# FFN up tiles: high and low parts of the input side by side in one matmul of 512 columns

## What is computed

```python
def conv_ffn(h, w_up, conv_w, conv_b, w_down):      # w_up 1024 x 5632, w_down 2816 x 1024
    u = dwconv(h @ w_up, conv_w, conv_b)            # depthwise over tokens, 3 taps, zero padded
    gate, val = jnp.split(u, 2, axis=-1)
    return (jax.nn.silu(gate) * val) @ w_down

lat = lat + g2 * conv_ffn(hl, ffn_w_up, ffn_conv_w, ffn_conv_b, ffn_w_down)
```

## Time and profile before

| | |
|---|---|
| median of 3 runs | 872.07 us |
| the profiled execution | 871.97 us, of it the span from first to last instruction 870.2 us |
| FFN stage: first up matmul to the start of the last down tile | 276.9 to 465.0 us of the span |
| TensorE busy | 859.8 us, 99% of the span |
| VectorE busy | 657.1 us, 76% |
| ScalarE busy | 488.6 us, 56% |
| DMA | 160.9 MB, 185 GB/s on average |

### The profile page before, as it was taken

How to read it: one execution, slowest core, us unless ns; L and a number is a source line. 1 busy time by engine, 2 the same in 40 slices (tenths; PEclk the granted TensorE clock), 3 DMA queues, 4 the chain that set the end, 5 groups by cost and what they waited for, 6 DMA issues and landing times.

```text
span 870.2 us, 16530 instructions
## 1 busy us (share of the span) xinstructions
PE 859.8 (99%) x6054; PEld 768.5 (88%) x6054; DVE 657.1 (76%) x1118; ACT 488.6 (56%) x774; POOL 0.2 (0%) x4
## 2 busy tenths in 40 slices
PE   8999999999999999999999999999999999999997
PEld 3688888888899999999998899999998888888886
DVE  4793899999997788877668797766577767666665
ACT  5433677777765654555557545555545555444444
POOL 0000000000000000000000000000000000000000
PEclk9999999999999999999999999999999999999999
DMA  9974444444446657556564554444465456555551
GB/s 346 408 290 154 148 144 147 145 145 145 165 153 237 193 201 249 177 199 192 170 196 142 199 189 147 152 164 147 145 218 168 128 192 214 193 193 183 181 191 49
DMA packets 45441, 160.90 MB, mean 185 GB/s; under 512 B 5200, under 2 KB 6608, under 8 KB 45264
## 3 DMA queue, kind: packets, MB, share of 16 engines
q1 hardware_dynamic: 43488, 156.43, 52.7%
q10 hardware_dynamic: 1904, 3.81, 1.2%
HBM read 159.16 MB, written 1.05 MB: 184 GB/s over the span
## 4 chain that ended last, share of the span: by engine, by line
PE 93%; DVE 3%; ACT 2%; DMA 1%; issue 1%; SPq 1%; DVEq 0%; ACTq 0%
PE bank L418 19%; PE bank L420 18%; PE bank L419 18%; PE bank L439 6%; PE bank L483 5%; PE bank L485 5%; PE bank L484 5%; PE bank L440 3%; PE bank L1232 2%; PE bank L1236 2%; PE bank L1240 2%; DMA arena<-in_ada 1%; PE bank L451 1%; PE bank L1358 1%; PE bank L1201 1%
## 5 line engine op out<-in xcount | busy, mean ns | idle before, releaser
L412 DVE TENSOR_TENSOR w_lo<-raw,w_hi 128x1024 fp32r<-128x1024 f32 x244 | 295.1, 1223 | 100.9 <-ACT w_hi L405 100.7
L405 ACT ACTIVATE w_hi<-raw 128x1024 fp32r<-128x1024 f32 x244 | 252.7, 1051 | 92.2 <-PE bank L420 45.1
L418 PE MATMUL bank<-h_both,w_hi 128*128 128x256 f32 (+1 forms) x928 | 281.2, 303 | 0.0
L419 PE MATMUL bank<-h_both,w_hi 128*128 128x256 f32 (+1 forms) x928 | 276.2, 298 | 0.0
L420 PE MATMUL bank<-h_both,w_lo 128*128 128x256 f32 (+1 forms) x928 | 275.9, 297 | 0.0
L418 PEld LDWEIGHTS bank<-h_both,w_hi 128*128 128x128 f32 x928 | 174.4, 188 | 8.2 <-issue 1.3
L420 PEld LDWEIGHTS bank<-h_both,w_lo 128*128 128x128 f32 x928 | 175.0, 189 | 5.7
L419 PEld LDWEIGHTS bank<-h_both,w_hi 128*128 128x128 f32 x928 | 174.8, 188 | 5.2
L418 PE MATMUL bank<-y_hi,w_hi 128*128 128x256 f32 x304 | 87.0, 286 | 0.1
L419 PE MATMUL bank<-y_lo,w_hi 128*128 128x256 f32 x304 | 85.6, 281 | 0.0
L420 PE MATMUL bank<-y_hi,w_lo 128*128 128x256 f32 x304 | 85.5, 281 | 0.0
(11 more groups left out here) (283 smaller groups left out, 1194.9 us busy)
## 6 DMA issues: line engine op xcount, KB each, us to landing
raw<-in_stream SPq DMA_DIRECT2D x244, 512.0 KB, 3.4
arena<-in_ada SPq DMA_DIRECT2D x40, 512.0 KB, 7.2
xres<-in_ada SPq DMA_DIRECT2D x8, 512.0 KB, 3.3
tok<-in_tok SPq DMA_DIRECT2D x4, 512.0 KB, 5.4
con<-in_con ACTq DMA_DIRECT2D x1, 1472.0 KB, 6.2
xres<-in_tok ACTq DMA_DIRECT2D x1, 1024.0 KB, 8.4
out<-arena SPq DMA_DIRECT2D x4, 256.0 KB, 2.0
arena<-in_post_mix ACTq DMA_DIRECT2D x1, 512.0 KB, 4.1
```

The lines of the kernel that those rows point to most:

```text
L405: act.activation(w_hi[c.slot][:, :], raw[c.slot][:, :], ACT.Copy).then_inc(S("split_hi"), 1)
L412: dve.tensor_tensor(w_lo[c.slot][:, :], raw[c.slot][:, :], w_hi[c.slot][:, :].bitcast(F32), ALU.subtract).then_inc(S("split_lo"), 1)
L418: pe.matmul(dst, hi_w, a_hi, start=start, stop=False, skip_group_check=True)
L419: pe.matmul(dst, hi_w, a_lo, start=False, stop=False, skip_group_check=True)
```

## The change

The up tiles of steps 1 to 21 use `apart_tile`; those of step 0 put their low products into the right half of the bank. ScalarE copies the right half to SBUF (`z_low`), VectorE adds the left half from PSUM to it (`z_f`), and both the convolution's starter on ScalarE and VectorE's taps read `z_f` from SBUF. TensorE's wait before up(j) is for the adds of tile j - 2, one for each half. The gate sums follow the steps 2, 4, ..., 16, and 18 steps are written out. SP issues the fifth to the eighth gate load behind the stream groups 3, 5, 7 and 8.

```diff
-GATE_ROWS = (0, 0, 1, 1, 1, 1, 1, 1, 1, 1)
+GATE_ROWS = (0, 0) + (1, 0) * 8
-FFN_PEEL = 10
+FFN_PEEL = 18
+GATE_GROUPS = (3, 5, 7, 8)
@@ arena
+        z_low = [part(T) for _ in range(2)]
+        z_f = [part(T) for _ in range(2)]
+        used[0] = TC + 8 * T
@@ SP
-            for u in range(1, 5):
+            for u in range(1, 9):
                 load_stream(i_ffn + u)
-                for k in (2 * u - 2, 2 * u - 1) if u >= 3 else ():
-                    load_gate(k)
-            with sp.Fori(i_ffn + 5, N_ALL // RING) as i:
+                if u in GATE_GROUPS:
+                    load_gate(4 + GATE_GROUPS.index(u))
+            with sp.Fori(i_ffn + 9, N_ALL // RING) as i:
                 load_stream(i)
@@ ScalarE, ffn_tile
-                act.wait_ge(S("multiplied"), n_done)
+                for half in range(2):
+                    act.wait_ge(S("multiplied"), n_done + half - 1)
+                    if has_old:
+                        act.wait_ge(S("z_full"), t * 2 + half - 1)
+                    act.activation(z_low[half], psum[4 + 2 * half + p][:, T:2 * T], ACT.Copy).then_inc(S("z_low"), 1)
                 if has_old:
                     act.wait_ge(S("u_full"), t - 1)
                 for half in range(2):
-                    act.activation(conv[p][half], psum[4 + 2 * half + p][:, 0:T], ACT.Identity,
+                    act.wait_ge(S("z_full"), t * 2 + (1 + half))
+                    act.activation(conv[p][half], z_f[half], ACT.Identity,
                                    scale=p1("conv_w", t + (2 * JF + half * JF)),
                                    bias=p1("conv_b", t + half * JF)).then_inc(S("conv_mid"), 1)
@@ TensorE, ffn_up
                 if has_old:
-                    pe.wait_ge(S("conv"), j * 2 - 2)
-                column_tile(pe, c[0], psum[4 + p][:, 0:T], T, T)
-                column_tile(pe, c[1], psum[6 + p][:, 0:T], T, T)
+                    pe.wait_ge(S("z_full"), j * 2 - 3)
+                apart_tile(pe, c[0], psum[4 + p])
+                if has_old:
+                    pe.wait_ge(S("z_full"), j * 2 - 2)
+                apart_tile(pe, c[1], psum[6 + p])
@@ VectorE, ffn_tile
                 for half in range(2):
-                    z = psum[4 + 2 * half + p]
+                    dve.wait_ge(S("z_low"), t * 2 + (1 + half))
+                    dve.tensor_tensor(z_f[half], psum[4 + 2 * half + p][:, 0:T], z_low[half], ALU.add).then_inc(S("z_full"), 1)
+                for half in range(2):
                     x = conv[p][half]
                     dve.wait_ge(S("conv_mid"), t * 2 + (1 + half))
-                    dve.scalar_tensor_tensor(x[:, 1:T], z[:, 0:T - 1], p1("conv_w", t + half * JF), x[:, 1:T],
-                                             ALU.mult, ALU.add).then_inc(S("conv_left"), 1)
+                    dve.scalar_tensor_tensor(x[:, 1:T], z_f[half][:, 0:T - 1], p1("conv_w", t + half * JF), x[:, 1:T],
+                                             ALU.mult, ALU.add).then_inc(S("conv"), 1)
```

More of the change, by code:

```diff
@@ L993, in ffn_tile @@
                     between()
-                act.wait_ge(S("conv"), t * 2 + 2)
+                act.wait_ge(S("conv"), t * 4 + 4)
                 act.activation(f_silu[p], conv[p][0], ACT.Silu).then_inc(S("f_silu"), 1)
@@ L1450, in ffn_up @@
                 if first:
-                    first_columns_late(pe, c, [psum[4][:, 0:T], psum[6][:, 0:T]], 2 * KT)
+                    first_columns_late(pe, c, [psum[4][:, 0:T], psum[6][:, 0:T]], 2 * KT, [psum[4][:, T:2 * T], psum[6][:, T:2 * T]])
                     return
                 if has_old:
-                    pe.wait_ge(S("conv"), j * 2 - 2)
-                column_tile(pe, c[0], psum[4 + p][:, 0:T], T, T)
-                column_tile(pe, c[1], psum[6 + p][:, 0:T], T, T)
+                    pe.wait_ge(S("z_full"), j * 2 - 3)
[3 more added lines that the diff above has]
+                apart_tile(pe, c[1], psum[6 + p])
             def ffn_down(t, s, c, first, last):
@@ L2037, in ffn_tile @@
                 for half in range(2):
-                    z = psum[4 + 2 * half + p]
+                    dve.wait_ge(S("z_low"), t * 2 + (1 + half))
+                    dve.tensor_tensor(z_f[half], psum[4 + 2 * half + p][:, 0:T], z_low[half], ALU.add).then_inc(S("z_full"), 1)
+                for half in range(2):
                     x = conv[p][half]
                     dve.wait_ge(S("conv_mid"), t * 2 + (1 + half))
-                    dve.scalar_tensor_tensor(x[:, 1:T], z[:, 0:T - 1], p1("conv_w", t + half * JF), x[:, 1:T],
-                                             ALU.mult, ALU.add).then_inc(S("conv_left"), 1)
+                    dve.scalar_tensor_tensor(x[:, 1:T], z_f[half][:, 0:T - 1], p1("conv_w", t + half * JF), x[:, 1:T],
+                                             ALU.mult, ALU.add).then_inc(S("conv"), 1)
                 for half in range(2):
-                    z = psum[4 + 2 * half + p]
                     x = conv[p][half]
-                    dve.wait_ge(S("conv_left"), t * 2 + (1 + half))
-                    dve.scalar_tensor_tensor(x[:, 0:T - 1], z[:, 1:T], p1("conv_w", t + (4 * JF + half * JF)), x[:, 0:T - 1],
+                    dve.wait_ge(S("conv"), t * 4 + (1 + half))
+                    dve.scalar_tensor_tensor(x[:, 0:T - 1], z_f[half][:, 1:T], p1("conv_w", t + (4 * JF + half * JF)), x[:, 0:T - 1],
                                              ALU.mult, ALU.add).then_inc(S("conv"), 1)
-                dve.wait_ge(S("conv"), t * 2 + 2)
+                dve.wait_ge(S("conv"), t * 4 + 4)
                 dve.wait_ge(S("f_silu"), t + 1)
```

## The result

| | before | after |
|---|---|---|
| median | 872.07 us (871.95 to 872.6, 4 runs) | 888.52 us (888.21 to 890.79, 4 runs) |
| ratio after / before | | 1.0194, 95% interval 1.018 to 1.0207 |
| the profiled execution | 871.97, span 870.2 | 890.79, span 889.0 |
| start of down(21) in it | 465.04 | 481.30 |

The change costs 16.4 us, 1.9%. The forecast was 884.8 with a range of 879 to 890: the direction and the mechanism were right, the size 3.7 us short.

The account below looks back on a forecast made before the run. TensorE's matmuls bound the kernel, but VectorE with ScalarE would become slower: 22 tiles at 1.14 us hide TensorE's 3.4 us gain and start the last down tile 12.8 us later. 871.97 + 12.8 = 884.8 us, range 879 to 890.

Parts of the forecast that it names:

- up(j): The two up tiles of FFN step j on TensorE; expected to wait on VectorE's low parts from about step 3 on.
- down(21): The last FFN down tile on TensorE; forecast to start at 477.8 instead of 465.04, 12.8 us later.
- the ring: VectorE and ScalarE's ordered chain between closing subtractions; forecast 8.6 us a plain step, 9.8 with gate sum, over TensorE's 8.48.
- close(j-2) - 0.6: Earliest stall-free start of step j's up tiles: 0.6 us before VectorE's closing subtraction of tile j-2.
- d: Time added per FFN tile by VectorE's adds and the starters now waiting for them: 1.14 us, over 22 tiles.
- close(21): VectorE's closing subtraction of the last FFN tile; forecast at 477.3, against 463.87 before the change.
- upper bound of 1.25: Highest d considered, in us a tile: a starter of 0.65 and hand-overs twice as long.
- lower bound 0.79: Lowest d considered, in us a tile: only the two adds' issue on VectorE, starters hidden.
- rival C: ScalarE's convolution starters stay hidden, d is 0.79, 7.7 us less: 877.1 us; chance 5%.
- rival B: VectorE's taps get shorter reading SBUF, 0.425 each, 4.4 us less: 880.4 us; chance 6%.
- rival A: TensorE stays the bound in the FFN, adds and starters fall into waits, only -3.4 us remains: 868.6 us; chance 8%.
- rival D: TensorE's clock falls in the wait before the last down tile, up to 2.9 us more there: about 888; chance 12%.

Follow-up runs that it names:

- three_matmuls: The changed kernel with three matmuls of 256 columns in place of one of 512 and one of 256: 889.59 us.
- wait_moved: The changed kernel with ScalarE's wait for u_full moved from between the low-half copies and the starters to ahead of the copies: 887.96 us.
- adds_ahead: The changed kernel with ScalarE's low-half copies and VectorE's two adds moved ahead of the step's second weight chunk: 876.29 us.
- spread_only: The kernel before with only the gate sums spread to steps 2 to 16, their loads moved and 18 steps written out: 872.19 us.
- short_sums: The changed kernel with each gate sum on 8 of its 1024 columns, waits and loads kept: 881.70 us.
- pieces: The changed kernel with each gate sum cut into four pieces of 256 columns, put where VectorE waits for ScalarE: 880.53 us.

## Why the prediction was right, and where it was short

**The bound and the ring.** Right. That VectorE with ScalarE had been as slow as TensorE in steps with a gate sum was read from 8.67 against 8.64, and the equal closing subtractions of `three_matmuls` show that the new ring doesn't feel TensorE at all. The rule for up(j), close(j-2) - 0.6, names the wait that came: TensorE's waits for L416 sum to 10.2 us, up to 1.5 each. Of the 3.7 us that were missing 3.5 lie in the ring: down(21) starts at 481.30 where 477.8 was foretold.

**The term that was mis-sized: d.** The prediction had 1.14 us a tile, the trace shows 8.75 - 7.48 = 1.27. The starter itself was right (0.598 for the 0.60 taken):

```profile
L998 ACT ACTIVATE arena<-arena,par x44: 586/598/605, 286.8 to 476.9; 128x256 f32<-128x256 f32 x44
L2054 DVE SCALAR_TENSOR_TENSOR arena<-arena,par x44: 483/484/486, 287.4 to 477.5; 128x255 f32<-128x255 f32 x44
```

The rest is in the hand-overs. Add to first tap takes 1.15 instead of 1.08; `wait_moved` shows 0.06 of it to be the wait for u_full between copies and starters, which had long been fulfilled. And the second tap follows the first by 0.50 (the pair 0.98 less 0.48) instead of 0.45, as starters reading SBUF come 0.50 apart (1.10 less 0.60) and not 0.45. Together 0.12 to 0.13, times 22 some 2.8 us. The other 0.7 of the ring's 3.5 (close(21) at 480.82, 477.3 foretold) are a start 0.1 later, a single starter 0.29 longer on its way, at 323 us, and four steps in the loop that take 8.75 like the others, where the prediction's 7.41 would have given 7.41 + 1.27 = 8.68. Why that starter was late and why the loop's 0.07 is lost no run tells. The upper bound of 1.25 for d was below the truth: its terms had no room for a further wait ahead of the starters.

**Two adds back to back.** The lower bound 0.79 was built on the cadence of the taps; adds come 0.33 apart and two take 0.67. In the prediction this touched only rival C; it also made the expectation of `adds_ahead` too high.

**The copies of the low half, banks, SP's queue, gate sums.** Cost nothing, as said. For the sums' places and SP's queue `spread_only` shows it. Behind the copies ScalarE still idles 1.52 us ahead of the starters, and among TensorE's waits there is none for an add (L2050). That the sums cost what they take on the ring is shown by `short_sums` and `pieces`.

**Taps from SBUF (rival B).** 0.484 against 0.476 from PSUM: not shorter. (By the fixed costs that the Trainium skill gives in VectorE: DVE Perf Modes, the TRN2 errata, they would be an estimated 0.065 shorter; the trace doesn't agree for this operation.)

**TensorE stays the bound (rival A).** Refuted for this order of instructions, and true for another: with the adds ahead and the sums in the waits TensorE is the bound again, and the result is 869.62 for 868.6 worked out, the last tile being 0.8 of the difference. The way there was not the one that A named. The adds' part of d is 0.67, not under 0.40; but the sums' 9.1 us left the ring as well, so that its step of 8.15 fell under TensorE's 8.48. The argument against A, that nothing can be issued into the waits of an ordered queue, holds for an order that stays as it is. The programmer can change the order and put independent work ahead of a wait.

**The end of the stage.** 3.4 us between the end of down(20) and the start of down(21) were foretold; 3.5 came (477.81 to 481.30), 2.6 of them idle. TensorE's timeline after:

```profile
477.69 0.28 PE L424 MATMUL bank<-y_hi,w_lo 128*128 128x256 f32 x1
480.55 0.69 PE L1293 MATMUL bank<-con,arena 128*128 128x128 f32 x2 [2.58 <-ACT arena L1026]
481.30 0.58 PE L422 MATMUL bank<-y_hi,w_hi 128*128 128x256 f32 x1
```

The gate's columns (L1286) stand ahead of down(20) in the queue, not behind it. The instruction that waited at the end is not down(21) but the turn of the gate's rows (L1293): ScalarE's copy of these rows (L1026) stands in its queue behind y_hi of tile 21. It costs nothing: down(21) starts 0.48 behind close(21), where the prediction had 0.47.

**The clock (rival D).** Had 12%, and came in one run of four of the changed kernel and in all four of `three_matmuls` and `wait_moved`. It cost 2.3 us in the changed kernel and 2.6 at most (`pieces`, 881.83 against 879.28), for the foretold 2.9, and in most runs 1.1 to 1.5. (The Trainium skill, TensorE: Matmul & The Clock Gate, HAM oscillation, says that idle gaps throttle the clock; here the trace agrees, by the windows above.) Why it falls in one run and not in another with the same wait of 2.6 us is open; no run here tells it.

## What to carry to other kernels

Where two engines hand work back and forth, time the ring of their ordered instructions from one closing instruction to the next and compare it with the step of the bounding engine; a busy share of 76% says nothing when the idle time stands in waits in the middle of the queue. An operation that makes another wait for it costs its own time and that of the one it holds: before adding one, look for the place in the queue where its consumer runs beside something else. Independent work that takes 0.4 us of the queue fitted here into waits of 0.5 for nothing, so cut such work to the size of the waits.

## What the runs showed of the hardware that was not expected

- A second wait, long fulfilled, ahead of an instruction of ScalarE on the ring cost 0.06 us; moved ahead of other work it cost nothing (1.15 against 1.09 from add to tap).
- VectorE's adds of 256 columns with one source in PSUM follow each other by 0.33 us, its two-operation taps by 0.39.
- After 2.5 to 2.6 us without a matmul the clock was at its lower level for about 3.4 us in four traces and 6.8 in one, at a cost of 1.1 to 2.6 us; other runs of three of these kernels had no such cost. With the wait filled by matmuls of constants none of four runs had it.
